# A tenth place for expert weights, the branch ahead of the last scatter, and tokens' rows and experts' sums turned raw

## What is computed

```python
def first_block(x, mem, ...):
    h = rms_norm(x, norm_mix)                 # 256 x 1024
    zu, zv, zq, zk, zval = split(h @ w_in)    # w_in 1024 x 2560
    a_out = chunked_sgu(gelu(zu), gelu(zv), ...)
    o = diff_attention(zq, zk, zval, lam)     # 4 heads, two softmaxes each
    x = x + concat([a_out, rms_norm(o)]) @ w_out
    x = x + memory_attention(rms_norm(x, norm_xq), rms_norm(mem, norm_mem), ...)
    x = x + hierarchical_moe(rms_norm(x, norm_ffn), ...)   # 32 experts, top 2
    return rms_norm(x, norm_final)

def second_block(x, ...):
    u = rms_norm_2(x, norm_mix_pre)
    h = x + rms_norm_2(moba_attention(u, w_qkv, w_o), norm_mix_post)   # 8 heads
    u = squared_relu_mlp(rms_norm_2(h, norm_ffn_pre), w_up, w_down)    # d_ff 4096
    return h + rms_norm_2(u, norm_ffn_post)
```

## Time and profile before

| | |
|---|---|
| median of the runs | 1015.07 us (3 runs, 1014.17 to 1015.34) |
| profiled execution | 1013.95 us |
| its span | 1012.70 us, mean granted PE clock 0.986 |
| busy: PE, its weight loads, DVE, ACT, POOL | 94%, 65%, 44%, 36%, 3% |
| read from HBM | 287.90 MB, 285 GB/s over the span |
| chain that ended last | PE 79%, issue 6%, ACT 6%, DVE 5%, DMA 4%, POOL 1% |

### The profile page before, as it was taken

The page is one execution under the profiler, slowest core; times in us unless marked ns, Lnnn a source line. Parts: engine busy times, 40 slices in busy tenths (PEclk is TensorE's granted clock), DMA queues, the critical chain, the costliest instruction groups (busy, mean ns, idle before and its releaser), DMA issues.

```text
span 1012.7 us, 13539 instructions
## 1 busy us (share of the span) xinstructions
PE 956.6 (94%) x5353; PEld 653.8 (65%) x5353; DVE 441.1 (44%) x757; ACT 360.3 (36%) x593; POOL 26.2 (3%) x40
## 2 busy tenths in 40 slices
PE   6999989998999999999999999985999989999997
PEld 5979878985444444444444444332998879998886
DVE  5856555445232232222222222214564755555434
ACT  7635446433121121111111112114455544554332
POOL 1400000000000000000000000000000000000000
PEclk9989999998999999999999999999999989999999
DMA  9943443486899999999999999999645535555501
GB/s 319 361 146 126 167 164 134 161 316 264 311 430 421 429 428 426 427 429 428 429 428 430 428 428 428 428 428 362 212 156 165 167 107 164 180 192 172 205 1 42
DMA packets 72629, 289.66 MB, mean 286 GB/s; under 512 B 4993, under 2 KB 44545, under 8 KB 60546
## 3 DMA queue, kind: packets, MB, share of 16 engines
q1 hardware_dynamic: 72002, 288.79, 73.8%
q10 hardware_dynamic: 576, 0.17, 0.1%
HBM read 287.90 MB, written 1.05 MB: 285 GB/s over the span
## 4 chain that ended last, share of the span: by engine, by line
PE 79%; issue 6%; ACT 6%; DVE 5%; DMA 4%; POOL 1%; SPq 0%; ACTq 0%; DVEq 0%
PE bank L1519 21%; PE bank L433 11%; PE bank L434 11%; PE bank L435 11%; PE bank L1541 10%; PE bank L1493 4%; DMA ring<-in_w_up 3%; ACT w_high L494 3%; PE bank L1552 3%; DVE w_low L523 1%; DVE arena L2303 1%; PE bank L1530 1%; ACT hidden_high L2127 1%; PE bank L723 1%; PE bank L761 1%
## 5 line engine op out<-in xcount | busy, mean ns | idle before, releaser
L1519 PE MATMUL bank<-ring,arena 128*64 128x512 f32 x1024 | 228.7, 598 | 7.9 <-issue 7.1
L523 DVE TENSOR_TENSOR w_low<-ring,w_high 128x2048 fp32r<-128x2048 f32 x76 | 174.1, 2290 | 122.3 <-ACT w_high L494 122.3
L494 ACT ACTIVATE w_high<-ring 128x2048 fp32r<-128x2048 f32 x76 | 145.1, 1909 | 120.8 <-PE bank L435 120.7
L1519 PEld LDWEIGHTS bank<-ring,arena 128*64 128x64 f32 x1024 | 75.5, 137 | 140.9 <-issue 139.0
L1541 PE MATMUL bank<-ring,arena 128*64 128x512 f32 x512 | 116.9, 597 | 5.3 <-issue 5.3
L433 PE MATMUL bank<-xT_high,w_high 128*128 128x256 f32 x384 | 112.0, 292 | 2.6 <-DVE xT_low L532 1.8
L434 PE MATMUL bank<-xT_low,w_high 128*128 128x256 f32 x384 | 109.8, 286 | 0.0
L435 PE MATMUL bank<-xT_high,w_low 128*128 128x256 f32 x384 | 109.7, 286 | 0.0
L1644 DVE SCALAR_TENSOR_TENSOR y_low<-bank,arena,y_high 64x512 fp32r<-64x512 f32 x64 | 48.0, 750 | 139.3 <-ACT y_high L1584 138.8
L1584 ACT ACTIVATE y_high<-bank,arena 64x512 fp32r<-64x512 f32 x64 | 43.7, 683 | 135.3 <-PE bank L1541 134.9
L1571 ACT ACTIVATE arena<-bank 128x256 f32<-128x256 f32 x32 | 12.3, 385 | 191.1 <-PE bank L1519 191.1
(11 more groups left out here) (280 smaller groups left out, 1455.9 us busy)
## 6 DMA issues: line engine op xcount, KB each, us to landing
ring<-in_w_down SPq DMA_DIRECT2D x32, 2048.0 KB, 25.0
ring<-in_w_gate SPq DMA_DIRECT2D x31, 2048.0 KB, 21.3
ring<-in_w_up SPq DMA_DIRECT2D x31, 2048.0 KB, 25.8
ring<-in_w_up SPq DMA_DIRECT2D x16, 1024.0 KB, 5.6
ring<-in_w_down SPq DMA_DIRECT2D x16, 1024.0 KB, 5.0
ring<-in_attn_w_qkv SPq DMA_DIRECT2D x12, 1024.0 KB, 11.8
ring<-in_w_in SPq DMA_DIRECT2D x10, 1024.0 KB, 11.7
ring<-in_w_kv_mem SPq DMA_DIRECT2D x8, 1024.0 KB, 5.2
```

The source lines that it names most:

```text
L494: SC.activation(parts[buffer[0][u]][0][:, :], lanes[n % len(lanes)], ACT.Copy).then_inc(*high.inc(u))
L523: DVE.tensor_tensor(p[1][:, :], lanes[n % len(lanes)], p[0][:, :].bitcast(F32), ALU.subtract).then_inc(*split.inc(u))
L1519: last = PE.matmul(GU[t * SLOTS:(t + 1) * SLOTS, 0:NGU], xs[:, k, :], wgu[:, :, k, t * (DE // JT):(t + 1) * (DE // JT)], start=k == 0, sto ...
```

## The change

**Ring.** A tenth place of 2 MB (`extra_piece`), whose first 1024 columns are the gain rows' `bc`, holds the down weights of expert 3 and nothing else of the experts. From expert 4 on the ring is one place back: expert 4 has slots 8 (up), 1 (gate), 0 (down), expert 5 has 2, 3, 4, expert 6 has 5, 6, 7, and so on in threes. Expert 3's down weights are issued right behind its quarters; expert 4's up behind down(0), its gate and down behind gate_up(1); expert 5's gate behind down(1), its up and down behind gate_up(2); expert 6 alike. From expert 7 on the waits are those of before. The last expert's places and the second block's buffers (`parts2`) and first loads move with it. GpSimd's own DMA scratch is set to 2048 bytes.

**Start.** x is turned as it arrives; the norm's factor comes later: v by ACT's scale at the GELU, val by DVE's scalar, u, q and k by a product with a row of the factors (`features_out`, on DVE; GELU of u in a second step on ACT). The row is made by turning a widened column (`rh`, behind u0). u0 is loaded ahead of mem, u1 is multiplied ahead of mem's transposes, and mem's second half is split first.

**Second block.** The branch stands ahead of the last scatter, which is done behind it, with a signal of its own for tokens 0. ACT (z0, z1, z3) and DVE (z2) copy the sums to XN, PE turns them raw, ACT and DVE split them with norm_final's and the next norm's column gains multiplied; v0.1's low part is made before. The product with norm_final's row, the squares and both norms follow behind. v is scaled as it leaves its bank, q and k leave by DVE through the row of norms (`r1`, turned behind q0). norm_final comes as a column early and as a row late.

```diff
-hT00 hT01 hT10 hT11 +v.0 +v.1 -v.0 -v.1 u0@2 memT00@6 memT01@7 memT10@0 memT11@1 u1@3 q0@4 sguw@5 k0@2 +O0@6 +O1@7
+hT00 hT01 hT10 hT11 +v.0 +v.1 -v.0 -v.1 u0@2 rh@6 u1@3 memT00@6 memT01@7 memT10@0 memT11@1 q0@4 sguw@5 k0@2 +O0@6 +O1@7
-pT00@4 pT01@5 pT10@6 pT11@7 +v0.0 +v0.1 -v0.0 -v0.1 q0 k0 q1 s0 s1 k1 q2 t0 t1 s2 s3 k2 a0 a1
+pT00@4 pT01@5 pT10@6 pT11@7 +v0.0 +v0.1 -v0.0 -v0.1 q0 r1 k0 q1 s0 s1 k1 q2 t0 t1 s2 s3 k2 a0 a1
...
-    bc = nc.alloc_sbuf_tensor("gain_rows", [P, 1024], F32)
+    extra = nc.alloc_sbuf_tensor("extra_piece", [P, PIECE], F32)
+    bc = extra[:, 0:1024]
...
-        turn(bank1, "hT", [(rows_v.at(f"h{h}"), rows_s.at(f"h{h}")) for h in range(NH)])
+        turn(bank1, "hT", [(loads.after(f"x{h}", 1),) for h in range(NH)], src=X)
...
         f("u0", hT)
+        bank = open_bank(bank1, "rh")
+        for h in range(NH):
+            PE.wait_ge(*norm_wide.at(f"h{h}"))
+            last = PE.transpose(bank[:, h * P:(h + 1) * P], wide_h[:, h * P:(h + 1) * P], ident[:, :])
+        last.then_inc(*turned.inc("rh"))
+        f("u1", hT)
         turn(bank1, "memT", [(rows_v.at(f"mem{h}"), rows_s.at(f"mem{h}")) for h in range(NH)], src=memX)
-        f("u1", hT)
         f("q0", hT)
...
+        def features_out(u, dst, scale):
+            DVE.wait_ge(*unit1.at(u))
+            DVE.wait_ge(*bank1.freed("rh"))
+            DVE.scalar_tensor_tensor(out=dst, in0=banks[bank1.bank[u]][:, :].rearrange("p (n t) -> p n t", t=S),
+                                     scalar=scale, in1=row_h.rearrange("p (n t) -> p n t", n=1).to_broadcast([P, 2, S]),
+                                     op0=ALU.mult, op1=ALU.mult).then_inc(*bank1.inc(u))
...
         low("q0")
-        turned_lows(bank1, "memT", 0, memT, G_MEM)
+        features_out("u1", uT[:, 2:4, :], 1.0)
+        low("k0")
         turned_lows(bank1, "memT", 1, memT, G_MEM)
-        low("k0")
...
-        low("val.0")
...
+        features_out("q0", qT[:, 0:2, :], float(DQK) ** -0.5)
+        low("val.0")
+        features_out("k0", kT[:, 0:2, :], 1.0)
...
         diff_soft_b(3)
+        features_out("q1", qT[:, 2:4, :], float(DQK) ** -0.5)
         low("km0")
+        features_out("k1", kT[:, 2:4, :], 1.0)
...
+    def expert_loads(q, n, n0):
+        gate, up, dn = places_of(n0)
+        SP.wait_ge(*q.at("gate_up", n - 2))
+        if up < gate + 2:
+            load_piece(gate, expert_of(w_gate, n), place_sem[gate])
+            load_piece(up, expert_of(w_up, n), place_sem[up])
+        else:
+            load_piece(up, expert_of(w_up, n), place_sem[up])
+            load_piece(gate, expert_of(w_gate, n), place_sem[gate])
+        SP.wait_ge(*q.at("down", n - 2))
+        load_piece(dn, expert_of(w_down, n), place_sem[dn])
+    def places_of(n):
+        if n < 4:
+            w = (6 + 3 * n) % RING
+            return w, w + 1, EXTRA if n == 3 else w + 2
+        w = (5 + 3 * n) % RING
+        return (1, w, 0) if w + 1 == RING else (w, w + 1, w + 2)
...
+    def early_loads(n):
...
+        else:
+            first, second = ((gate, w_gate), (up, w_up)) if gate < up < gate + 2 else ((up, w_up), (gate, w_gate))
+            SP.wait_ge(*q.at("down", n - 3))
+            load_piece(first[0], first[1][n], place_sem[first[0]])
+            SP.wait_ge(*q.at("gate_up", n - 2))
+            load_piece(second[0], second[1][n], place_sem[second[0]])
+            load_piece(dn, w_down[n], place_sem[dn])
...
     spill = nc.values_load(spill_flag[0:1, 0:1], min_val=0, max_val=1)
-    scatter(q, NE, NE, LAST % 3, 0, False)
-    scatter(q, NE, NE, LAST % 3, 1, True)
...
+    tokens0_scattered = nc.alloc_semaphore("tokens0_scattered")
+    scatter(q, NE, NE, LAST % 3, 0, False, tokens0_scattered)
+    scatter(q, NE, NE, LAST % 3, 1, True)
...
+        SC.wait_ge(tokens0_scattered, 1)
+        z_copy(0)
+        z_copy(1)
         SC.wait_ge(*q.at("scattered", NE // 2))
-        part_squares("z", 0, ["z0", "z1"])
-        part_square("z", 1, 0, "z2")
-        z_squares(0)
-        part_square("z", 1, 1, "z3")
-        z_squares(1)
-        turned_highs(bank2, "pT", 0, xT2[0], G_PRE2)
-        turned_highs(bank2, "pT", 1, xT2[0], G_PRE2)
+        z_copy(3)
+        SC.wait_ge(*z_gained.at("columns"))
+        for c4 in range(2):
+            for h in range(NH):
+                turned_highs(bank2, "pT", h, xT2[0], G_PRE2, groups=(c4,))
+        for h in range(NH):
+            SC.wait_ge(*bank2.freed(f"z{2 * h}"))
+            SC.wait_ge(*bank2.freed(f"z{2 * h + 1}"))
+            z_squares("zr", h, XN, arena[3], small[:, 16 + 2 * h:17 + 2 * h])
+        SC.wait_ge(*z_gained.at(0))
+        z_squares("z", 0, X, arena[4], small[:, 20:21])
+        high("q0")
+        SC.wait_ge(*z_gained.at(1))
+        z_squares("z", 1, X, arena[4], small[:, 21:22])
...
-        high("q0")
         high("k0")
+        norm_row("r1")
         high("q1")
-        feature_out("q0", flat(q2T[:, 0:2, :]), QSCALE)
         high("k1")
-        feature_out("k0", flat(k2T[:, 0:2, :]))
...
```

363 lines of the change are left out of this document (209 added, 154 removed).

## The result

The changed kernel takes **1005.37 us** (median of 4 runs, 1004.59 to 1007.65); the kernel before took 1015.21 on the same chip (4 runs, 1014.17 to 1016.53). The ratio is 0.990, 95% interval 0.9882 to 0.9917: faster by 8.4 to 12.0 us. The prediction said 1006.2 in a range of 1002.5 to 1010.5, faster at 0.93. The sum was right. Several of its terms were not, and that they made up for each other is luck; most of what follows is about that.

What follows compares the result with a forecast made beforehand. PE was taken to bound the kernel outside the expert loop (with some waits), the weight stream within it. Terms -0.45 - 3.3 - 3.3 - 1.8 = -8.85 gave 1005.1 for the profiled execution, 1006.2 us as median, range 1002.5 to 1010.5.

Steps and rivals of the forecast that it cites:

- The tenth place: Expert weight ring: down 3 issued earlier gains 4.9 us, partly paid back at expert 7; -3.3 us, bounds -4.9 and 0.
- The start: First block: raw turning brings PE's first product 2.0 us earlier, -1.3 before k1's output, -0.45 after it.
- signs of being wrong: VectorE named as releaser of scores' or features' matmuls, or PE waiting on k0's parts beyond 722 (shifted).
- term 2: First block's start, raw turning of tokens' rows: -0.45 us, including 0.85 lost as k1's output leaves late by VectorE.
- The turn: Into the second block: v0's first product 6.2 us earlier; -3.3 us with the clock's fall, -5.2 at full clock.
- rival A: Turn into second block: the clock doesn't fall at v0, 5.2 instead of 3.3 us gained, 1004.3 us; chance 0.25.
- The bank: Second block, before v1.0: idle wait for k3's copy out of bank 5 goes; -1.8 us, bounds -1.8 and 0.
- At nothing: Gain column, u0 ahead of mem, low parts' order, ring one place on, smaller scratch: no cost, beside PE work.
- B: Expert ring: it pays all back, the extra piece only moving the stall to expert 7; 1009.5 us, chance 0.12.
- C: Turn at second block waits for another engine (branch, or VectorE's list before k0): gain nothing, 1009.5 us; chance 0.12.
- E: Expert ring: down 3's early issue is held by the quarter before it; equated with B, no separate chance given.
- D: Fourteen outputs moved to VectorE: it becomes the bound, 9.7 us on PE's path, +2.6, 1017.7 us; chance 0.03.

Runs made afterwards that it cites:

- e8: The changed kernel itself, unaltered, timed and profiled a second time: 1006.46 us, ratio 0.9915 to the kernel before.
- e4: Changed kernel plus useless transposes in PE's idle stretches before x lands, before v.0's first product and around the ranks: 1002.64 us, ratio 0.9880.
- e11: Changed kernel plus useless transposes in more idle stretches than e4, also before out2, last scatter and f0: 1007.94 us, ratio 0.9923.
- e2: Changed kernel with the first block's start put back as in the kernel before: 1007.38 us, ratio 0.9919.
- e6: Kernel before with one word of the bank list changed, k3 moved to bank 6: 1019.10 us, ratio 1.0034.
- e9: Kernel before with three banks pinned, k3 in 6, a2 in 7, a3 in 0: 1013.52 us, ratio 0.9977.
- e5: Changed kernel with the branch put back behind both last scatters: 1008.58 us, ratio 0.9930.
- e12: Changed kernel with idle stretches filled by useless transposes and the tenth place also used for expert 7's down weights: 1008.85 us, ratio 0.9924.

## Why the prediction came out, step by step

**What bounds the kernel: right.** PE outside the loop, the stream within it.

**The tenth place: right mechanism, wrong size.** Forecast -3.3, measured -1.3 in the two profiled executions, 0.9 to 2.1 over the traces without added work. Expert 31's start, forecast for 679.3, was 682.20. Down 3 was issued at 259.99 and landed 11.6 us later at 271.6 (forecast 269.8), down 4 at 286.6 (285.1), which is 3.4 instead of 4.9 us before the old one. The stream then led by 4.6 us at expert 6's last piece (316.2 against 320.7). The term that was mis-sized is the one at expert 7. I let its first piece land 7.8 us after its issue, since the earlier trace rows has that for a piece with nothing ahead of it, at 321.3, and kept 4.3 us. It landed 9.3 us after the issue:

```profile
DMA to landing us min/median/max: 9.3/9.3/9.3
```

The piece ahead of it landed at 316.2, 2.2 us after this issue, and from there it took 7.0 us, where a piece in a full queue takes 4.9. In e8 it was issued 2.7 us ahead of the end of the queue and landed 8.1 after it (10.8 after its issue). The one microsecond that I took off for this was 1.5 to 3. All traces together, for the pieces issued between 262 and 331 us (landing is the issue's start plus its time to landing):

| stream left at the issue (us) | lands behind the piece before (us) | pieces |
|---|---|---|
| none (0.2 to 0.4 too late) | 7.9 to 8.2 | 5 |
| 0.6 to 1.8, all down weights | 5.9 to 7.3 | 5 |
| 2.2 to 2.8 | 7.0 to 8.2 | 5 |
| 2.9 to 3.5 | 5.2 to 7.6 | 8 |
| 3.6 to 4.0 | 5.2 to 6.1 | 9 |
| 4.1 to 4.4 | 5.1 to 5.7 | 3 |
| 4.6 to 6.6 | 4.8 to 5.1, once 5.5 | 27 |

So a gate or up piece issued with 2.2 to 2.8 us of stream left comes as late as one issued into a dry stream, or nearly. That isn't a rule for every piece: the down weights in the second row came 7.7 to 7.9 us after their issue, as if nothing was ahead. The reason is open. In e4 and e11 the same piece found 3.9 and 3.1 us left and came 5.6 and 5.7 behind, which is where their extra microsecond comes from. Two more gaps of 0.7 and 0.8 us, at 343 to 348 and 388 to 393 us with a full queue, took the rest; other traces have such gaps elsewhere or not, and their cause is open.

**The start: right at its first row, then short by the clock.** -1.93 for -2.0; k1's output costs 0.68 for 0.85. What the prediction didn't have is that the clock is still low there: in this trace 4 us of products at half speed cost 1.8. In the trace -0.45 became +0.31, over all traces it is about -0.2, the ratios of e2 say a gain of 0.4 to 1.9. The two can both hold, since in other executions the clock rises earlier (8.8 in e8), and e11, with the full clock from 6.0 us on, has the scores of head 4 at 85.82, 1.2 us ahead of the kernel before. On the way from -2.0 to -1.3 the prediction names no row. And one of its signs of being wrong did appear, DVE as the releaser of the scores of head 4; term 2 had put a price on it, so it refutes nothing.

**The turn: right to 0.1 us where the clock allowed.** v0's first product came 6.19 us earlier relative to expert 31 (forecast 6.2), k0's 5.40 (forecast 5.2 at full clock; against 44.13 us in the kernel before the other traces of the new turn have 3.2 to 4.3). I took the fall of the clock that the earlier trace rows shows into the likeliest case, for -3.3; the profiled execution had none (-5.4: rival A in this term), e8 had half of it: (722.89 - 727.18) - (682.67 - 683.05) = -3.9. So the likeliest case and rival A were both partly so, and the choice between them should have been a mean of the two, not a choice. That this trace had no fall is luck; the ground for rival A that the runs bear out is another than the one it gave: shorter idle time, less of the fall.

**The bank: right.** -1.97 for -1.8 from k0 on; alone, 2.08 in the trace and 2.3 in the ratio. The mechanism is shown from both sides by e6 and e9.

**At nothing: right for the branch**, with a price of 1.3 us if its cover is gone (e5); the 3 us that the prediction gave branch and code fetch stands in no row, but the stalls in e11 and e12 are of that size and more. The other items at nothing weren't tried one by one.

**Sum.** Forecast -8.85, measured -9.4 in the spans. By terms: start +0.8 worse than forecast, place 2.0 worse, turn 2.1 better, bank 0.2 better, clock in places the change doesn't touch (134, 245, 815) together 0.9 better. What the place lost the turn's clock gave back, and another execution of the same kernel (e8) takes 1.8 us more. Of the rivals, B (all paid back) was nearer to the truth of its term than the forecast; C is out, the branch lies under cover; E is out, since down 3 was issued at 259.99, right behind the quarter; D is out, since DVE is busy 45% of the span, though it is the releaser at two places, as term 2 had it for one.

## What to carry to other kernels

A ring's extra place is worth what is left when its lead meets the next release that PE makes. In these traces a 2 MB piece of gate or up weights issued with 2.2 to 2.8 us of stream left came nearly as late as into a dry one, and only with 4.6 us or more, about a piece's time, was next to nothing lost.

Where banks are given in turn, ask who reads each bank last: one name moved in the list made this kernel 3.4 us slower, three pinned made it 2.3 us faster.

Time won ahead of a stretch in which the clock is still low can be lost whole: of 1.93 us at the first product 0.13 were left at u0 in one look, and 1.79 in another, where the clock rose earlier. Look at the pitch of the products behind the place where you win. The clock's state in one profiled execution is a sample; two looks at the same kernel differed by 1.8 us.

## What the hardware showed that was not expected

- Work of no use in PE's idle stretches made the kernel faster by 2.0 to 3.6 us in the ratios. The trace of e4 puts 1.5 of it down to the clock's fall around 245 us, which is gone; the earlier rise at the start (4.6 instead of 8.8 to 14.1 us) brought 0.2 us at u0, and 1.5 only with twice the work there (e11).
- Around 60 us the clock falls in every trace, for 6.8 or 10.2 us, filled or not, with PE busy throughout (6.84 of the 6.84 us ahead of it in the changed kernel): there it does products with a single row of weights between others (L719 with 1x128). Idle time isn't the only thing that brings it down; what does it there wasn't tried.
- Behind a branch that isn't taken PE had its next instruction after 1.29 us (when a scatter had gone before), 3.50 and 3.69 (right behind the down products), and then, some instructions on, stood for another 4.38 and 5.33 us. Whether it is the amount of code between the branch and the first urgent instruction wasn't tried.
